# Attention by token tile with the output product and the router between its steps

## The reference, cut to what matters

```
h = rms_norm(x, ln1_g); proj = h @ w_in          # 2304 columns: q1 q2 k1 k2 v conv ssm
for each of 4 heads, causal, with a relative bias:
  p = softmax(q1 k1' / 8 + bias) - lam * softmax(q2 k2' / 8 + bias);  a = p @ v
a = rms_norm(a, subln_g) * (1 - lam_init)
c = silu(layer_norm(causal depthwise conv of 31 taps over a GLU of the conv columns))
s = GLU(gelu(complex diagonal state space scan of the ssm columns))
x = x + concat[a, c, s] @ w_out                   # 1024 x 1024
h2 = rms_norm(x, ln2_g)
group logits (4) and expert logits (32) of h2; top 1 group, top 2 experts in it
x = x + sum over the chosen experts of gate * (silu(h2 w_gate) * (h2 w_up)) w_down
out = rms_norm(x, final_g)
```

## Time and profile before

| | us |
|---|---|
| median of 3 runs (1385.89 to 1394.44) | 1391.37 |
| the profiled execution, its own time | 1393.03 |
| its span | 1390.8 |
| PE busy in the span | 1238.4 (89%) |
| DVE / ACT / POOL busy | 532.5 / 354.2 / 260.3 |
| TensorE's granted clock, mean of the span | 0.907 of full |

### The profile page before, as it was taken

The page is one execution under the profiler, slowest core; times in us unless marked ns, Lnnn a source line. Parts: engine busy times, 40 slices in busy tenths (PEclk is TensorE's granted clock), DMA queues, the critical chain, the costliest instruction groups (busy, mean ns, idle before and its releaser), DMA issues.

```text
span 1390.8 us, 16297 instructions
## 1 busy us (share of the span) xinstructions
PE 1238.4 (89%) x5013; PEld 604.6 (43%) x5014; DVE 532.5 (38%) x1207; ACT 354.2 (25%) x714; POOL 260.3 (19%) x218
## 2 busy tenths in 40 slices
PE   5999999999999796999728999999899999999950
PEld 5896444455755553455422333333233333333310
DVE  3450079503768863122272222222222222222217
ACT  3121100013556543000002222222232222222212
POOL 1010499500010111000002111111111111111113
PEclk9999999975669867999858999999999999999985
DMA  7225010040000004522516729999969998989327
GB/s 229 21 39 117 31 31 31 0 196 5 1 1 31 1 0 167 196 91 91 206 66 248 308 109 379 380 418 420 419 275 383 396 419 362 419 354 418 140 84 291
DMA packets 83971, 270.33 MB, mean 194 GB/s; under 512 B 25716, under 2 KB 46884, under 8 KB 59332
## 3 DMA queue, kind: packets, MB, share of 16 engines
q1 hardware_dynamic: 46884, 242.76, 44.4%
q0 software_dynamic: 8320, 16.80, 3.3%
q10 hardware_dynamic: 28704, 9.98, 2.8%
HBM read 253.25 MB, written 26.74 MB: 201 GB/s over the span
## 4 chain that ended last, share of the span: by engine, by line
PE 77%; DVE 9%; DMA 6%; issue 3%; ACT 2%; SPq 1%; ACTq 1%; POOL 0%; POOLq 0%; DVEq 0%
PE psum L1215 24%; PE psum L1234 12%; PE psum L975 12%; PE psum L1153 8%; PE psum L1107 4%; PE psum L972 3%; DMA W<-in_w_gate 3%; PE psum L1203 2%; PE psum L970 2%; PE psum L1128 1%; PE psum L1222 1%; DMA h_rows<-RD 1%; DMA W<-in_x 1%; DVE smx L1453 1%; DVE W L1450 1%
## 5 line engine op out<-in xcount | busy, mean ns | idle before, releaser
L1215 PE MATMUL psum<-W,RD 128*64 x800 | 367.3, 602 | 11.7 <-DVE RD L1690 11.7
L1216 PE MATMUL psum<-W,RD 128*64 128x512 f32 x800 | 367.3, 603 | 0.0
L1215 PEld LDWEIGHTS psum<-W,RD 128*64 128x64 f32 x800 | 106.3, 138 | 222.1 <-issue 216.2
L1234 PE MATMUL psum<-W,RD 128*64 x400 | 184.0, 603 | 2.6 <-ACT RD L904 2.6
L1235 PE MATMUL psum<-RD 128*64 128x512 f32 x400 | 184.0, 603 | 0.0
L1671 DVE TENSOR_TENSOR RD<-psum,RD 128x256 f32<-128x256 f32 x50 | 21.3, 425 | 413.5 <-ACT RD L900 413.5
L975 PE MATMUL psum<-W 128*128 128x512 f32 x384 | 165.2, 592 | 0.0
L651 POOL DMA_INDIRECT y_rows<-RD,tabi x49 | 52.2, 1065 | 472.4 <-ACT RD L911 462.7
L1107 PE MATMUL psum<-W 64*128 64x512 f32 (+3 forms) x192 | 103.1, 676 | 14.9 <-ACT W L827 12.8
L1153 PE MATMUL psum<-W,RD 128*128 128x512 f32 x256 | 114.1, 604 | 1.1 <-ACT RD L810 1.1
L975 PEld LDWEIGHTS psum<-W 128*128 128x128 f32 x384 | 72.9, 190 | 91.1 <-issue 91.1
(11 more groups left out here) (318 smaller groups left out, 1440.2 us busy)
## 6 DMA issues: line engine op xcount, KB each, us to landing
W<-in_w_up SPq DMA_DIRECT2D x32, 2048.0 KB, 12.8
W<-in_w_gate SPq DMA_DIRECT2D x32, 2048.0 KB, 17.8
W<-in_w_down SPq DMA_DIRECT2D x32, 2048.0 KB
W<-in_w_in SPq DMA_DIRECT2D x9, 1024.0 KB, 9.0
W<-y_rows SPq DMA_DIRECT2D x16, 512.0 KB, 9.4
W<-in_x SPq DMA_DIRECT2D x8, 512.0 KB, 10.6
xr<-in_x ACTq DMA_DIRECT2D x8, 512.0 KB, 4.3
x_rows<-W SPq DMA_DIRECT2D x8, 512.0 KB, 3.8
```

Of the source, the lines that this page charges most:

```text
L1215: pe.matmul(bank(2)[0:HALF].rearrange("p (g n) -> p g n", g=2), x, near, start=k == 0, stop=k == KD - 1)
L1216: ins = pe.matmul(bank(2)[HALF:P], x, upgate1[:, k].rearrange("p g n -> p (g n)"), start=k == 0, stop=k == KD - 1)
L1234: pe.matmul(out[0:HALF], a, W[:, bass.ds(base + (2 * KD * FF + D * k), 512)], start=k == 0, stop=k == FK - 1)
```

## The change

1. **Attention goes by token tile.** Item k is tile k // 4, head k % 4, from the first tile (128 keys) up. Of the `w_in` chunks for q and k each now holds two heads of both maps, loaded in 4 transfers of 64-column pieces, so that in `qkT` the two maps of a head lie in the two halves of the partitions.
2. **A longer loop.** One loop of 46 steps holds everything from the first score product to the last logits. In each step PE issues `scores(k, 0)`, the first part of `turn(k - 2)`, `scores(k, 1)`, `fill(k, 0)`, the second part of the turn, `fill(k, 1)`, `times_v(k - 3)`. A fill is two products of 512 columns: in steps 0 to 3 those of the last two units, in steps 8 to 39 those of the output product, four steps to a tile, all in PSUM bank 7, half a row at a time, the half added by DVE (`x2_half`) before the next half begins. Steps 4 to 7 have no fill. Per tile, at fixed distances, stand the transposes of the heads, the transposes of h2 and the logits.
3. **The state space output moves up.** PE runs units up to number 44, the convolution's transposes, `y`, unit 45, then 8 more small jobs, then the loop with units 46 and 47 in it. ACT takes the convolution's result out behind unit 43 and not behind unit 47.
4. **Less on DVE.** The bias of far keys is folded into the band, so two small operations per map go; map 1 is no longer divided by its sum but the quotient goes into one factor and into ACT's copy of the output, so one pass over the probabilities goes (L1475). The probabilities have 3 buffers for map 1 and 2 for map 2.
5. **Transfers.** SP's queue issues x, x2 and h2 too, tile by tile; slot 0's down weights and slot 1 are issued behind tile 5's h2, slot 2's up and gate weights behind tile 7's h2.

The rest of the program (routing, experts, last stage) is as before.

```diff
 CHUNKS = [(1024, "v"), (2048, "ssm"), (1280, "v"), (1792, "gate"), (1536, "a"),
-          (0, "qk"), (256, "qk"), (512, "qk"), (768, "qk")]
+          (0, "qk"), (128, "qk"), (512, "qk"), (640, "qk")]
...
+EARLY_UNITS = len(UNITS) - 2
+MISC = ([("conv_to_tok", i) for i in range(4)] + [("ssm_to_ch", i) for i in range(4)]
+        + [("conv_to_ch", i) for i in range(4)] + [("glu", i) for i in range(4)] + [("head", i) for i in range(NT)])
+FIRST_HEAD = MISC.index(("head", 0))
+NI = HEADS * NT
+ITERS = 4 * (NT - 1) + 18
+def parts(k):
+    return 1 if k // HEADS < 4 else 2
...
+def tile_at(k, off):
+    t, r = divmod(k - off, HEADS)
+    return t if r == 0 and 0 <= t < NT else None
...
+def unit_bank(u):
+    return 4 + u % 4 if u < EARLY_UNITS - 2 else 6 if u == EARLY_UNITS - 2 else 7
+def misc_bank(n):
+    return 4 + n % 2 if n < 12 else 5
...
+        pT = [RG[:, 1024 * q:1024 * q + 1024].rearrange("p (k n) -> p k n", k=KD) for q in range(2)]
+        x2 = RG[:, 2048:5120].rearrange("p (t n) -> p t n", t=3)
+        h2T = RG[:, 5120:6144].rearrange("p (k n) -> p k n", k=KD)
+        xa = RG[:, 6144:8192].rearrange("p (t n) -> p t n", t=2)
...
+        p1 = [RE[:, 0:1024], RE[:, 1024:2048], xr[:, :]]
+        p2 = [RE[:, 2048:3072], RE[:, 3072:4096]]
...
+            sp.wait_ge(unit_ps, LAST_UNIT[len(CHUNKS) - 2] + 1)
+            sp.dma_start(wout[:, 0:4], wo[:, 0:4]).then_inc(wout_in[0], 16)
...
+            sp.wait_ge(misc_ps, 12)
+            sp.dma_start(wout[:, 6:8], wo[:, 6:8]).then_inc(wout_in[2], 16)
+            sp.dma_start(rw[:, :, 0:4], t["group_router_w"][0].rearrange("(k p) n -> p k n", p=P)).then_inc(rw_in, 16)
+            sp.dma_start(rw[:, :, 4:36], t["expert_router_w"][0].rearrange("(k p) n -> p k n", p=P)).then_inc(rw_in, 16)
+            load_x(0)
+            load_x(1)
+            sp.wait_ge(unit_ps, len(UNITS))
+            sp.dma_start(wout[:, 4:6], wo[:, 4:6]).then_inc(wout_in[1], 16)
             load_up(0)
             load_gate(0)
             for i in range(NT):
+                sp.wait_ge(x2_ok, 2 * i + 2)
+                sp.dma_start(x2_dram[i * P:(i + 1) * P, :], x2[:, i % 3, :]).then_inc(x2_out[i % 3], 16)
+                if i + 2 < NT:
+                    load_x(i + 2)
+                sp.wait_ge(h2_ok, i + 1)
+                sp.dma_start(h2_dram[i * P:(i + 1) * P, :].rearrange("p (k n) -> p k n", k=KD),
+                             mixT[:, :, i * P:(i + 1) * P]).then_inc(h2_out, 16)
+                if i == 5:
+                    sp.wait_ge(o_ps, NI)
+                    load_down(0)
+                    load_up(1)
+                    load_gate(1)
+                    load_down(1)
+                    sp.dma_start(fgb, t["final_g"].rearrange("(o d) -> o d", o=1).to_broadcast([P, D])).then_inc(fg_in, 16)
             load_up(2)
             load_gate(2)
...
+            for u in range(LAST_UNIT[3] + 1, EARLY_UNITS - 2):
                 evac(u)
             act.wait_ge(set_in, 16 * SET_N)
             for c in range(2):
                 act.wait_ge(conv_ps, c + 1)
                 act.activation(convo[:, c, :], banks(2 - 2 * c, 2), ACT.Identity, bias=convb[:, c:c + 1]).then_inc(conv_ev, 1)
+            evac(EARLY_UNITS - 2)
...
+            act.wait_ge(y_ev, 4)
+            act.activation(RG[:, 6144:8192], RG[:, 6144:8192], ACT.Gelu_apprx_tanh).then_inc(gelu_ok, 1)
+            evac(EARLY_UNITS - 1)
+            for n_ in range(4, 12):
+                misc(n_)
...
+            act.wait_ge(conv_ok, 4)
+            for k in range(ITERS):
+                if 4 <= k < NI + 4:
+                    o_evac(k - 4)
+                if 2 <= k < NI + 2:
+                    p_evac(k - 2, 0)
                 if k < NI:
+                    exps(k, 0)
+                if 2 <= k < NI + 2 and parts(k - 2) == 2:
+                    p_evac(k - 2, 1)
+                if k < NI:
+                    exps(k, 1)
+                if k < 2:
+                    misc(12 + 2 * k)
+                    misc(13 + 2 * k)
+                if k in (1, 3):
+                    evac(EARLY_UNITS + k // 2)
+                i = tile_at(k, 8)
+                if i is not None:
+                    misc(FIRST_HEAD + i)
+                i = tile_at(k, 12)
+                if i is not None:
+                    act.wait_ge(x2_ok, 2 * i + 2)
+                    act.activation(mixT[:, :, i * P:(i + 1) * P], x2[:, i % 3, :].rearrange("p (c n) -> p c n", c=KD),
+                                   ACT.Square, accum_out=ms2[:, i:i + 1]).then_inc(ms2_ok, 1)
...
-            for u in range(LAST_UNIT[3] + 1, len(UNITS)):
+            for u in range(LAST_UNIT[3] + 1, EARLY_UNITS - 1):
                 unit(u)
...
+            pe.wait_ge(conv_ev, 2)
+            for n_ in range(4):
+                misc(n_)
             pe.wait_ge(scan_ok, 1)
...
+            pe.wait_ge(set_in, 16 * SET_N)
+            unit(EARLY_UNITS - 1)
+            for n_ in range(4, 12):
+                misc(n_)
...
+                if i == 4 and h == 0:
+                    pe.wait_ge(unit_ev, len(UNITS))
                 for b in range(0, nk, 512):
                     w = min(512, nk - b)
+                    half = slice(DK * m, DK * m + DK)
+                    ins = pe.matmul(psum[:, 2 * m + b // 512, 0:w], qkT[half, h, i * P:(i + 1) * P],
+                                    qkT[half, HEADS + h, b:b + w], start=True, stop=True)
                 ins.then_inc(s_ps, 1)
...
+            def turn(k, part):
+                i = k // HEADS
+                if part == 0:
+                    pe.wait_ge(p_ok, k + 1)
+                if k or part:
+                    pe.wait_ge(pT_ev, parts_before(k) + part)
+                for c in range(4 * part, min(4 * part + 4, i + 1)):
+                    ins = pe.transpose(bank(4)[:, P * (c % 4):P * (c % 4) + P], p1[k % 3][:, c * P:(c + 1) * P], ident[:, :])
                 ins.then_inc(pT_ps, 1)
...
+            def fill(k, part):
+                if k < 4:
+                    unit(EARLY_UNITS + k // 2, 4 * (k % 2) + 2 * part, 2)
+                elif 8 <= k < 8 + 4 * NT:
+                    i, step = (k - 8) // 4, (k - 8) % 4
+                    half, own = step // 2, step % 2 == 1
+                    if k == 8 and part == 0:
+                        for s in range(3):
+                            pe.wait_ge(wout_in[s], 16)
+                        pe.wait_ge(conv_ok, 4)
+                        pe.wait_ge(ssm_ok, 1)
+                    if part == 0 and own and half == 0:
+                        pe.wait_ge(misc_ev, FIRST_HEAD + i + 1)
+                    if part == 0 and not own and 2 * i + half:
+                        pe.wait_ge(x2_ok, 2 * i + half)
+                    for q in range(2):
+                        c = (0 if own else 4) + 2 * part + q
+                        ins = pe.matmul(bank(7), mixT[:, c, i * P:(i + 1) * P], wout[:, c, 512 * half:512 * half + 512],
+                                        start=c == 4, stop=c == 3)
+                    if own and part == 1:
+                        ins.then_inc(proj_ps, 1)
+            def h2_turn(i, b):
+                if b == 0:
+                    pe.wait_ge(h2_ok, i + 1)
+                    pe.wait_ge(misc_ev, FIRST_HEAD + min(i + 2, NT))
+                else:
+                    pe.wait_ge(h2T_half, i + 1)
+                if i:
+                    pe.wait_ge(lg_ok, i)
+                for c in range(4):
+                    ins = pe.transpose(bank(5)[:, P * c:P * c + P], mixT[:, 4 * b + c, i * P:(i + 1) * P], ident[:, :])
+                ins.then_inc(h2T_ps, 1)
+            def logits(i):
+                pe.wait_ge(h2T_ok, i + 1)
+                pe.wait_ge(misc_ev, FIRST_HEAD + min(i + 3, NT))
+                if i == 0:
+                    pe.wait_ge(rw_in, 32)
+                for c in range(KD):
+                    ins = pe.matmul(bank(5)[:, 0:36], h2T[:, c, :], rw[:, c, :], start=c == 0, stop=c == KD - 1)
+                ins.then_inc(lg_ps, 1)
...
+            for k in range(ITERS):
                 if k < NI:
                     scores(k, 0)
+                if 2 <= k < NI + 2:
+                    turn(k - 2, 0)
                 if k < NI:
                     scores(k, 1)
+                fill(k, 0)
+                if 2 <= k < NI + 2 and parts(k - 2) == 2:
+                    turn(k - 2, 1)
+                fill(k, 1)
+                if 3 <= k < NI + 3:
+                    times_v(k - 3)
+                if k < 2:
+                    misc(12 + 2 * k)
+                    misc(13 + 2 * k)
+                i = tile_at(k, 8)
+                if i is not None:
+                    misc(FIRST_HEAD + i)
+                for b in range(2):
+                    i = tile_at(k, 14 + b)
+                    if i is not None:
+                        h2_turn(i, b)
+                i = tile_at(k, 17)
+                if i is not None:
+                    logits(i)
...
+            dve.wait_ge(ud_ok, 1)
+            y_add(0)
```

(81 more changed lines are left out.)

460 lines of the change are left out of this document (158 added, 302 removed).

## The result

The changed kernel takes **1311.72 us** (median of 4 runs, 1311.15 to 1313.01) against 1388.63 for the kernel before in the same session (4 runs, 1381.18 to 1394.44): a ratio of 0.945, 95% interval 0.940 to 0.950. The forecast was 1318, the range 1285 to 1362. The profiled execution took 1312.15, its span is 1309.6, so 81.2 less than the span before where 73.1 were forecast. The sum hit, but two of its terms were off by 13 and 15 us in opposite directions.

A forecast was written before the change was run, and what follows sets the result against it. PE was taken as the bound, losing 58 us to the low clock and 28 idle in attention. Routing starting 73.1 us earlier took the span from 1390.8 to 1317.7, so 1318 forecast, range 1285 to 1362.

The forecast's parts named there:

- unit 44 ends: Before the loop: unit 47's old end, 293.1, less three units of 6.87, so 272.5 us.
- y: State space output before the loop: stays at the low clock, 29.9 us as now; at full clock one half, 15.
- unit 45: Unit behind y: 6.9 us of work plus 1.7 for a start at the low clock.
- Rival A: y before the loop runs at the full clock; gain 15 + 1.7 us, so 1301; chance 27%.
- The loop's work: PE work in the loop at full clock: scores, times_v, turns, output product, logits, small jobs, two units; 271.9 us.
- The extras: Loop time not under its work: GLU, first step, steps 4 to 7, climbs, step waits, half adds, end; 30.7 us.
- Rival B: Low clock survives in the loop, through two stretches after steps 4 to 7: 34 us more, 1352; chance 12%.
- The end: Loop's end, last product to routing: h2 3.5, transposes and copies 2.5, logits 3.6, adding 0.2; 9.8 us.
- C: Attention's score, maximum, exponential chain is not covered, 2 us in each of 28 steps: 56 more, 1374; chance 7%.
- D: Wide steps 20 to 31 run at 1.2 GHz: up to 118 us more, 1436, slower than before; chance 3%.
- F: One PSUM bank for the output product: all 16 halves wait for DVE's add, 0.85 each; 1329; chance 7%.
- Transfers: Last h2 store, expert weights and small-piece q and k loads cost 0; late weights would cost 11 us more.

The follow-up runs named there:

- The first experiment: Kernel before, with ScalarE (ACT) taking the convolution's result out behind unit 44's turn instead of behind unit 47: 1368.51 us, ratio 0.989.
- paired kernels: Changed kernel with both maps' score products together, alternating by 512 keys (1270.08 us) or one map behind the other (1270.84); alternating with GLU products moved later: 1271.68.

## Why the prediction was right, and where its terms were not

The mechanism was right: fills cover attention's chain and hold the clock up. The product moved behind attention costs 45 us, and PE is busy in all of 350 to 558. The number is in part luck: the loop started 22.8 us earlier than forecast and took 15.2 longer. Term by term:

| term | forecast | measured |
|---|---|---|
| unit 44 ends | 272.5 | 268.8 |
| four convolution jobs | 2.9 | 2.4 |
| y | 29.9 | 16.8 |
| unit 45 | 8.6 | 6.9 |
| eight jobs | 10.9 | 7.1 |
| loop starts | 324.8 | 302.0 |
| loop to routing | 302.6 | 317.8 |
| routing starts | 627.4 | 619.75 |
| rest of the span | 690.3 | 689.9 |

- **Unit 44** is 3.7 early; the projection was so from its first tiles on. The first experiment, in which PE's program is that of before, ends unit 47 at 291.0 where the trace of before has 293.1, so some 2 us of this come and go with the execution, and I can't say whether the rest belongs to the change.
- **y was the wrong choice between two values**, the step "this is the first choice, and I take 29.9". Rival A (27%) is what happened, 13 us in y and 1.7 in unit 45. My argument was that the 2.9 us of jobs are a stutter like the wait of 2.79. They aren't: PE's longest pause in them is 0.30 us. The run with the wait put back shows both outcomes, so after 2.7 us of waiting it is uncertain, after 0.3 it stayed up in all seven traces that have it. The 16 transposes ahead of y did not bring it down either: 1.00 from 262.30 to 302. The price of a low start for unit 45, 1.7, was too high: where one occurred, in the run with the wait put back, it cost 1.0. Rival A's number, 1301, did not come out since the loop took back 15.
- **The loop's work** was forecast at 271.9. Measured: 317.8, of which PE idle 2.1 + 0.4 + 10.1 = 12.6 and lost to the clock at most 20 × 0.41 + 208 × 0.02 + 62 × 0.08 = 17.3 (stages above); 287.9 of work is left. The 16 missing are mostly the four changes between 64 and 128 rows: 0.40 us in the step shown, 12.8 if each of 32 steps pays it, an estimate. In the earlier trace rows an item's scores stand in one block of eight, so what its two changes cost is spread within the 3.63 us; cut in two with a turn between them, they cost it twice, and I had multiplied rates only.
- **The extras** of 30.7 came out as 29.9 but are made up otherwise. PE's idle time is 12.6 where I had some 25: the step waits (5.7) did not occur, and single halves waited 4.1 where I had 3. The clock cost up to 17 where I had 4 for two climbs and some at the logits. **Rival B**, the low level in the loop, came true to a third: one stretch, 334 to 350, and a short one. Steps 4 to 7 took 329.30 to 341.61, 12.3, as forecast, but by luck: PE waited 0.4 us in them and not 6, its work at full clock was 2.2 us a step and not 1.6 (329.30 to 331.52), and two thirds of the time ran at 1.2 GHz (clock 0.67). The mean clock of the whole loop is 0.95, right at the mark below which the prediction would have called itself failed.
- **The end** took 12.5 from the last product (607.28) to the routing, not 9.8: the last h2 goes out 4.7 behind the product and not 3.5, and tile 6's logits stand ahead of tile 7's transposes, which wait 1.60 for VectorE.
- **C, D, F** stayed out: no group of waits above 4.1 us, wide steps at 0.98, the single bank hidden.
- **Transfers** cost nothing, as assumed. The q and k loads of 256 KB in 256-byte pieces land in 4.3 us each (row of the page, below), far inside the cover. The 8 MB in front of the last h2 go out from 582.99 on, 29 us ahead of it where some 25 were forecast, and the rest of the span is as long as forecast, so no weights came late.

```profile
W<-in_w_in SPq DMA_DIRECT2D x16, 256.0 KB, 4.3
```

Where the gain comes from, by starts of the routing (700.52 before, 619.75 now, 80.8 us): 15.6 are y and the wait ahead of it, 10.3 the wait for the store, and some 31 the fills. Some 24 are left for the rest: the order by token tile, the longer pipeline, the two small operations per map, and a projection that ends some us earlier. No run takes these apart, so which of them counts is open; the removed pass is at most 3 of it.

What neither the prediction nor its rivals saw is a further sum: with the two maps in different halves, 42 us more were to be had by leaving their products together. The row that hints at it stands at step 0, where no turn comes between the maps: four instructions in the time that two take at a later step.

```profile
301.99 0.49 PE L1160 MATMUL psum<-W 64*128 64x128 f32 x4
...
319.39 0.48 PE L1160 MATMUL psum<-W 64*128 64x128 f32 x2
```

## What to carry to other kernels

A stage that alternates between engines can pay twice, in idle time and in TensorE's clock; independent products between its steps brought back both here, and they also hid a single PSUM bank. When two products contract over 64 rows each, put them in different halves of the partitions and right behind each other: here four transposes between them cost the whole overlap, and a change between 64 and 128 rows cost some 0.1 us more. Where a stage runs at either clock, look at the pauses ahead of it, but don't expect them to tell all: one of 2.70 us brought the clock down in one of five runs, one of 1.47 (the first experiment) stood ahead of a low stretch, five of 2.3 together ahead of the loop, none above 0.79, did not, and at 334 us it fell behind pauses of 0.22 and 0.20 only.

## What the runs showed of the hardware

- Two fp32 products over 64 rows in different halves of the partitions take the time of one: 1.93 us for 1024 keys of both maps. They need not alternate; two and two overlap as well.
- In the changed kernel the clock fell once with PE busy throughout, and no wait in sight. PE's row just before, then short stretches of it:

```profile
490.40 1.87 PE L1225 MATMUL psum<-rw,W 128*128 128x36 f32 x16
...
492.00:496.00 4.00, 4.00 (x13) 2.08 (x13) 2.13 (x6) 0.95 (x3) 0.00 (x0) 0.74 0.05 15
496.00:500.00 4.00, 4.00 (x6) 1.47 (x5) 1.57 (x6) 0.91 (x4) 0.00 (x0) 0.50 0.00 0
500.00:504.00 4.00, 4.00 (x17) 2.25 (x16) 1.37 (x2) 1.75 (x5) 0.00 (x0) 0.91 0.00 0
```

  It costs about 3 us. Three more traces of kernels with separate score products have one such fall (the copy put back, the extra VectorE pass, the GLU products later in the changed kernel), and in all four it comes 1.5 to 2 us behind the 16 narrow products of a tile's logits. The traces of the three paired kernels have none in 350 to 517. Its cause is open.
- A wait of 2.7 us ahead of y brought the clock down in one of five runs of the same kernel, at a cost of 15 us. Only that run has a trace; that the clock held in the four others is read from their times and mean clocks.
